# Blending the two attention maps on TensorE while they are turned, with the output scaling on VectorE

## The reference

```python
def diff_attend(q, k, v, lam_full):
    """q (B,H,2,Q,d), k (B,H,2,K,d), v (B,H,K,dv): (softmax1 - lambda softmax2) V."""
    s = jnp.einsum('bhmqd,bhmkd->bhmqk', q, k) * DIFF_QK_DIM ** -0.5
    p = jax.nn.softmax(s, axis=-1)
    return jnp.einsum('bhqk,bhkd->bhqd', p[:, :, 0] - lam_full * p[:, :, 1], v)
```

## Time and profile before

| | us |
|---|---|
| median of 3 runs (lowest, highest) | 2056.52 (2053.64, 2057.24) |
| the profiled execution, its own time | 2056.58 |
| its span from first to last instruction | 2054.9 |
| busy: PE / PEld | 1994.0 (97%) / 1689.9 (82%) |
| busy: DVE / ACT / POOL | 1284.4 (63%) / 759.7 (37%) / 115.2 (6%) |
| mean granted TensorE clock | 0.986 |

### The profile page before, as it was taken

How to read it: one execution, slowest core, us unless ns; L and a number is a source line. 1 busy time by engine, 2 the same in 40 slices (tenths; PEclk the granted TensorE clock), 3 DMA queues, 4 the chain that set the end, 5 groups by cost and what they waited for, 6 DMA issues and landing times.

```text
span 2054.9 us, 27752 instructions
## 1 busy us (share of the span) xinstructions
PE 1994.0 (97%) x10253; PEld 1689.9 (82%) x10255; DVE 1284.4 (63%) x1840; ACT 759.7 (37%) x996; POOL 115.2 (6%) x173
## 2 busy tenths in 40 slices
PE   9999999998999899999999999999999999899998
PEld 7888888885788889888888888888887887788886
DVE  6877678765547875877577753452345642556666
ACT  5322222345545333332222342222235433736453
POOL 1010001000003200000001000000000000000000
PEclk9999999999999999999999999999999999999999
DMA  8455455531120003555555432342234322043553
GB/s 346 168 195 183 169 186 175 173 113 62 42 72 20 1 22 103 194 184 173 180 192 175 159 114 97 102 169 102 72 109 168 144 102 82 21 144 143 180 188 123
DMA packets 52650, 274.80 MB, mean 134 GB/s; under 512 B 6128, under 2 KB 7472, under 8 KB 34256
## 3 DMA queue, kind: packets, MB, share of 16 engines
q1 hardware_dynamic: 33024, 203.97, 28.3%
q0 software_dynamic: 18960, 68.88, 9.9%
q10 hardware_dynamic: 576, 0.69, 0.1%
HBM read 272.47 MB, written 1.05 MB: 133 GB/s over the span
## 4 chain that ended last, share of the span: by engine, by line
PE 90%; DVE 5%; ACT 3%; issue 1%; DVEq 0%; ACTq 0%
PE ps L1021 15%; PE ps L1022 15%; PE ps L1023 15%; PE ps L1033 8%; PE ps L1248 6%; PE ps L1249 6%; PE ps L1247 6%; PE ps L1034 4%; PE ps L2413 2%; PE ps L2414 2%; PE ps L2415 2%; DVE w_lo L683 1%; PE ps L1900 1%; PE ps L1912 1%; PE ps L1908 1%
## 5 line engine op out<-in xcount | busy, mean ns | idle before, releaser
L683 DVE TENSOR_TENSOR w_lo<-w_raw,w_hi 128x2048 fp32r<-128x2048 f32 (+3 forms) x206 | 420.9, 2043 | 217.7 <-ACT w_hi L462 217.2
L1021 PE MATMUL ps<-h_parts,w_lo 128*128 128x512 f32 (+1 forms) x1424 | 538.6, 378 | 5.9 <-DVE h_parts L842 4.4
L1023 PE MATMUL ps<-h_parts,w_hi 128*128 128x512 f32 (+1 forms) x1424 | 535.7, 376 | 0.0
L1022 PE MATMUL ps<-h_parts,w_hi 128*128 128x512 f32 (+1 forms) x1424 | 535.7, 376 | 0.0
L462 ACT ACTIVATE w_hi<-w_raw 128x2048 fp32r<-128x2048 f32 (+3 forms) x207 | 353.9, 1710 | 477.0 <-PE ps L1249 254.0
L691 DVE SCALAR_TENSOR_TENSOR ada_product<-ada_w,silu_c 128x1024 bf16<-128x1024 f32 x256 | 313.2, 1223 | 20.3 <-DVE ada_product L691 10.3
L1021 PEld LDWEIGHTS ps<-h_parts,w_lo 128*128 128x128 f32 x1424 | 269.8, 189 | 55.9 <-DVE w_lo L683 5.0
L1023 PEld LDWEIGHTS ps<-h_parts,w_hi 128*128 128x128 f32 x1424 | 269.8, 189 | 48.3
L1022 PEld LDWEIGHTS ps<-h_parts,w_hi 128*128 128x128 f32 x1424 | 269.8, 189 | 47.5
L474 ACT ACTIVATE sil<-ps 128x512 f32<-128x512 f32 x66 | 39.5, 598 | 480.5 <-PE ps L1023 480.5
L1247 PE MATMUL ps<-hid_parts,w_lo 128*128 128x512 f32 x468 | 182.1, 389 | 0.0
(11 more groups left out here) (338 smaller groups left out, 2566.9 us busy)
## 6 DMA issues: line engine op xcount, KB each, us to landing
w_raw<-in_w_up SPq DMA_DIRECT2D x88, 1024.0 KB, 4.8
ada_w<-in_ada POOLq DMA_DIRECT2D x128, 512.0 KB, 3.6
w_raw<-in_w_down SPq DMA_DIRECT2D x32, 768.0 KB, 4.2
w_raw<-in_w_down SPq DMA_DIRECT2D x32, 640.0 KB, 3.9
w_raw<-in_w_ret_t SPq DMA_DIRECT2D x16, 1024.0 KB, 4.8
w_raw<-in_w_ab SPq DMA_DIRECT2D x14, 1024.0 KB, 4.8
ada<-in_ada SPq DMA_DIRECT2D x8, 1024.0 KB, 24.7
w_raw<-in_w_ret SPq DMA_DIRECT2D x8, 1024.0 KB, 4.8
```

Source lines behind the costliest of these rows:

```text
L683: dve.tensor_tensor(w_lo[parts_of(s, slot)][:, 0:elems], w_raw[slot][:, 0:elems], w_hi[parts_of(s, slot)][:, 0:elems].bitcast(F32), ALU.su ...
L1021: pe.matmul(out, lo, rhs_hi(k), start=first and k == 0, stop=False)
L1022: pe.matmul(out, hi, rhs_lo(k), start=False, stop=False)
L1023: mm = pe.matmul(out, hi, rhs_hi(k), start=False, stop=last and k == nk - 1)
```

## The change

The mix of the two maps moves from VectorE into TensorE's turning: where VectorE made `at_mixed` and TensorE transposed it, VectorE now makes a 128 by 128 matrix `at_share`, the identity times the factor (one column per query row), and TensorE forms for each 128 keys `probs0^T x identity + probs1^T x share` as two float32 products into one accumulator. `at_probs` gets a third buffer. The output scaling moves from ScalarE to VectorE, four turns behind the scores. The lambda sum stands one `diff` step earlier on VectorE. The splits of `S_AB + 1` leave the last `diff` step: the high part is made in turn 2 of the attention, the low part behind the attention; both parts of `S_AB + 2` are made behind it too. TensorE's wait for all outputs moves into `pe_decay_sums`, at the fifth step of `conv`.

```diff
-    at_probs = [put(f"at_probs{i}", [P, 2, T], at=at_r + 4 * KB * i)[0] for i in range(2)]
-    at_mixed = [put(f"at_mixed{i}", [P, T], at=at_r + (8 + 2 * i) * KB)[0] for i in range(2)]
+    at_probs = [put(f"at_probs{i}", [P, 2, T], at=at_r + 4 * KB * i)[0] for i in range(3)]
+    at_share = [put(f"at_share{i}", [P, P], at=at_r + 48 * KB + 512 * i)[0] for i in range(2)]
...
             if n >= 3:
                 pe_weigh_values(pe, n - 3)
-        pe.wait_ge(attn_out, len(ATTN))
+        pe.wait_ge(probs_done, len(ATTN))
...
     def pe_turn_probs(pe, n):
         nk = ATTN[n][2]
-        pe.wait_ge(mixed_done, n + 1)
+        pe.wait_ge(share_done, n + 1)
         if n >= 2:
             pe.wait_ge(pt_done, n - 1)
         for kt in range(nk // P):
-            mm = pe.transpose(ps[:, 5 + n % 2, kt * P:(kt + 1) * P], at_mixed[n % 2][:, kt * P:(kt + 1) * P], ident)
+            for m, share in enumerate((ident, at_share[n % 2][:])):
+                mm = pe.matmul(ps[:, 5 + n % 2, kt * P:(kt + 1) * P], at_probs[n % 3][:, m, kt * P:(kt + 1) * P], share,
+                               start=m == 0, stop=m == 1)
...
@@ act_diff @@
-            if n == 4:
-                split_hi(act, S_AB + 2, S_AB % 2, ELEMS[S_AB + 2])
+            if n == 2:
+                split_hi(act, S_AB + 1, (S_AB + 1) % 2, ELEMS[S_AB + 1])
...
-                if n >= 2:
-                    act.wait_ge(mixed_done, n - 1)
+                if n >= 3:
+                    act.wait_ge(turned_done, n - 2)
...
-            if n >= 3:
-                h, qt, nk = ATTN[n - 3]
-                act.wait_ge(pv_done, n - 2)
-                act.activation(df_o[:, qt, h, :], ps[:, (4, 7)[(n - 3) % 2], 0:P], ACT.Copy,
-                               scale=attn_n[:, (n - 3) % 4, 6:7]).then_inc(attn_out, 1)
...
@@ dve_diff @@
+            if n >= 4:
+                h, qt, nk = ATTN[n - 4]
+                dve.wait_ge(pv_done, n - 3)
+                dve.tensor_scalar(df_o[:, qt, h, :], ps[:, (4, 7)[n % 2], 0:P], attn_n[:, n % 4, 6:7], None, ALU.mult) \
+                   .then_inc(attn_out, 1)
...
-                dve.scalar_tensor_tensor(out=mixed[:, 0:nk], in0=probs[:, 1, 0:nk], scalar=st[:, 0:1],
-                                         in1=probs[:, 0, 0:nk], op0=ALU.mult, op1=ALU.add).then_inc(mixed_done, 1)
+                dve.tensor_scalar(at_share[(n - 1) % 2][:], ident, st[:, 0:1], None, ALU.mult).then_inc(share_done, 1)
...
-            if n == 5:
-                split_lo(dve, S_AB + 2, S_AB % 2, ELEMS[S_AB + 2])
...
@@ act_ab @@
-            split_hi(act, s + 2, slot, ahead)
+            if r < 5:
+                split_hi(act, s + 2, slot, ahead)
...
         act_diff(act)
+        split_hi(act, S_AB + 2, S_AB % 2, ELEMS[S_AB + 2])
...
@@ dve_ab @@
             if r == 4:
                 dve_low_ab16(dve)
-            else:
+                dve_lambda(dve)
+            elif r < 4:
                 split_lo(dve, s + 2, slot, ahead)
-            if r < 4:
                 dve_rope_diff(dve, r)
         walk(dve, "diff", body, unrolled=True)
-        dve_lambda(dve)
         dve_diff(dve)
+        for s in (S_AB + 1, S_AB + 2):
+            split_lo(dve, s, s % 2, ELEMS[s])
```

More of the change, by code:

```diff
@@ L1368, in build @@
     scores_done, max_done, probs_done = sem("scores_done"), sem("max_done"), sem("probs_done")
-    mixed_done, turned_done, pt_done = sem("mixed_done"), sem("turned_done"), sem("pt_done")
+    share_done, turned_done, pt_done = sem("share_done"), sem("turned_done"), sem("pt_done")
     pv_done, attn_out = sem("pv_done"), sem("attn_out")
@@ L1444, in act_diff @@
                 act.wait_ge(max_done, n + 1)
-                if n >= 2:
-                    act.wait_ge(mixed_done, n - 1)
+                if n >= 3:
+                    act.wait_ge(turned_done, n - 2)
                 for m in range(2):
-                    last = act.activation(at_probs[n % 2][:, m, 0:nk], ps[:, 2 * (n % 2) + m, 0:nk], ACT.Exp,
+                    last = act.activation(at_probs[n % 3][:, m, 0:nk], ps[:, 2 * (n % 2) + m, 0:nk], ACT.Exp,
                                           bias=st[:, 2 + m:3 + m], scale=0.125, accum_out=st[:, 4 + m:5 + m])
@@ L1501, in dve_diff @@
         order_v.wait_by(dve)
-        for n in range(len(ATTN) + 1):
+        for n in range(len(ATTN) + 4):
             if n < len(ATTN):
@@ L1511, in dve_diff @@
                 dve.tensor_scalar(st[:, 2:4], st[:, 0:2], -0.125, None, ALU.mult).then_inc(max_done, 1)
-            if n >= 1:
-                nk, st, probs, mixed = ATTN[n - 1][2], attn_n[:, (n - 1) % 4], at_probs[(n - 1) % 2], at_mixed[(n - 1) % 2]
+            if n >= 4:
[3 more added lines that the diff above has]
+                   .then_inc(attn_out, 1)
+            if 1 <= n <= len(ATTN):
+                st = attn_n[:, (n - 1) % 4]
                 dve.wait_ge(probs_done, n)
@@ L1686, in act_df_norm @@
         act.wait_ge(attn_out, len(ATTN))
-        act.wait_ge(mixed_done, len(ATTN))
+        act.wait_ge(turned_done, len(ATTN))
         act.activation(df_sq[:], df_heads, ACT.Square).then_inc(df_squared, 1)
@@ L1740, in pe_decay_sums @@
         pe.wait_ge(gates_ready, 1)
+        pe.wait_ge(attn_out, len(ATTN))
         for n, m in enumerate((C_TRIF, C_TRIB, C_ONE)):
```

## The result

The changed kernel takes 2060.21 us (median of 8 runs, 2058.86 to 2065.25) against 2056.64 for the kernel before beside it (8 runs): ratio 1.0021, 95% interval 1.0012 to 1.0031. The profiled execution took 2058.86 us, its span is 2057.2.

A forecast was written before the change was run, and what follows sets the result against it. TensorE was taken as the bound, time being won or lost where it idles or runs at lower clock. Stage +4.6 and half clock +1.7 make +6.3 us: 2062.8 us against the median (+0.3%), range 2058.0 to 2067.5.

The forecast's parts named there:

- head: Start of the differential attention: earlier value copies let TensorE's a/b projection end at 479.5 instead of 486.2, -6.7 us.
- first scores to last value product: TensorE's attention work summed from the projection's end, putting the last value product at 529.1 us against 526.8 before.
- gap before the convolution: After the last value product TensorE waits 2.7 us for a low part queued on VectorE behind the last output scaling.
- the stage: Differential attention, first scores to first convolution product, 52.9 us before; convolution to start at 531.8 instead of 527.25, +4.6 us.
- The blend: Mixing while turning on TensorE: 96 products, 192 records of 0.112 us, 22.2 us in all; 16 us more work.
- the fourth term: First convolution products, behind TensorE's 2.7 us idle: a half-clock stretch of 3.4 us, costing +1.7 us.
- rival A: At the gap before the convolution, the clock does not fall or falls harmlessly: +4.6 us, 2061.1 us; chance 0.22.
- A difference outside the stage: Sign of being wrong: before or behind the differential attention, the time differs; the forecast counted nothing there.
- VectorE's part of the first convolution step: Sign of being wrong: this work starts more than 12.7 us behind TensorE's start of that step.
- B: In TensorE's turning, an identity product costs one record like a transpose: not slower, 2054.1 or 2052.4 us; chance 0.12.
- C: In TensorE's products for turning, loads are exposed: 0.145 us a record, 6.3 us more, 2069.1 us; chance 0.06.
- D: At the attention's start, table load or lambda still precedes the copies, no early start: +6.7 us, 2069.5; chance 0.05.

The follow-up runs named there:

- the one without the blend: Changed kernel with VectorE mixing and TensorE transposing as before, output scaling still on VectorE; 2051.49 us against 2055.77 for the kernel before, ratio 0.9989.
- the second measurement: The changed kernel, unaltered, measured once more against the kernel before: 2062.15 us against 2055.77, ratio 1.0035.
- the blend alone: Kernel before plus only VectorE's share matrix, TensorE's two products in place of each transpose, and a third exponentials buffer; 2065.33 us against 2056.89, ratio 1.0036.
- the scaling alone: Kernel before with only the output scaling moved from ScalarE to VectorE, four turns behind; 2055.41 us against 2055.77, ratio 1.0002.
- the moves alone: Changed kernel with mix back on VectorE and scaling on ScalarE, keeping early value copies, late splits and moved wait; 2049.30 us against 2056.89, ratio 0.9958.

## Why the prediction was right or wrong

| term | forecast | measured |
|---|---|---|
| head: from first scores to the projection's end | -6.7 | -6.7 |
| first scores to last value product, in all | 54.7 | 54.75 |
| gap before the convolution | 2.7 | 2.69 |
| the stage, against before | +4.6 | +4.55 |
| half clock on the first convolution step | +1.7 | +1.4 and +1.6 in two traces of it |
| total | +6.3 | +3.6 and +6.4 in two measurements |

**Right by its own steps:** the stage. The head came as priced: TensorE idled 0.2 us and the clock stayed at 1.00. The blend came at 192 records of 0.112 us. Two parts of the sum erred against each other: a long blend took 1.89 us and a short one 0.99, so 23.0 and not 22.2 for all, and the value products 0.54 and 0.99 instead of 0.64 and 1.02, 12.2 and not 13.3, probably because the turned map is there early now and their first load is hidden. That the sum met 54.75 within 0.1 us is luck to that extent: the two errors are 0.8 and 1.1 us. The three waits for a share stand in the sum as 1.3 us, though 0.2, 0.2 and 0.8 make 1.2, and came as 1.4. The scaling takes 0.35 us instead of 0.29; it matters only once, in the tail.

**Where it was too sure:** the fourth term. A gap of 2.7 us was followed by half clock in both traces of the change, but not in the one without the blend, whose gap is as long to the hundredth. The row of 3.2 us from which I took it shows that such a gap can cost a fall, not that it does; rival A had its chance of 0.22 for a reason. The total of the first measurement, 3.6 us, is 2.7 below the forecast and inside the range. The traced execution does contain the fall, so this is not shown to be the missing term: the second measurement gave 6.4. What a total can tell here is bounded by half clock outside the stage, in the first 40 us above all.

Two signs that the prediction had named for being wrong did come. A difference outside the stage is in the traces: 1.8 us before it and about 2 behind it, none of which the sum has. And VectorE's part of the first convolution step came 14.1 us behind TensorE's start instead of 12.7; that sign was set too tight, since the forecast's own half clock on these products puts it there.

**The rivals.** A came in one of the three traces with the gap, but in the kernel without the blend and not in the change. B (a product against the identity costs one record) is out by the rows of L1419, identity and share alike. C is out: 0.112 us a record. The Trainium skill ("TensorE: Matmul & The Clock Gate", Back-to-back issue gap) gives about 81 ns for a 128-column product in a stream of load and product pairs, from which the prediction estimated 324 ns for a float32 product. The trace does not agree: a float32 product took 0.22 us in the blend as well. D is out: the table load stood at 462.98 us, 9.7 us ahead of the first copy. The work behind the stage stayed without price: VectorE had waited 1.98 us for its part of the first convolution step.

## What to carry to other kernels

Before work is moved to the engine that bounds a stage, compare it with the waits it removes: here 16 us of products took the place of some 8 us of waits, while a pipeline one turn longer gained 1.2 us a head without any work. And when a step is put behind a loop, look at what the loop's last turn waits for: a low part of 2.3 us was free behind the last mix and cost 2.7 us behind the last scaling.

## What the runs showed of the hardware that was not expected

- An idle stretch of TensorE of 5.2 us at the head of the stage was followed by half clock for 6.8 us in all three traces that have it (the kernel before, the blend alone, the scaling alone); the seven traces with 0.2 us there have none.
- Idle stretches of TensorE of 2.69 us were followed by half clock for 3.4 us in two traces (the change, twice) and by none in a third with the same gap. In the trace of the moves alone half clock came in a stage whose longest wait of TensorE was 1.0 us. What decides between the two is not shown.
- The clock in the first 40 us was 0.91 in one execution of the same program and 0.79 in another, and the first scores came 5.1 us apart.
